# Moving queries, a split output unit, fewer unread products and a finer last step in a two-block decoder kernel

## What is computed

```python
x = x + g1 * even_mixer(mod(rmsnorm(x)), mod(rmsnorm(ctx)))   # gated half + 8 heads over a window and the context
x = x + g2 * (relu(h @ w_ff1) ** 2 @ w_ff2)                   # "mlp 0"
x = x + g1 * conformer_conv(mod(rmsnorm(x)))                  # pw1, gate, 31 taps by depth, layernorm, pw2
x = x + g2 * (relu(h @ w_ff1) ** 2 @ w_ff2)                   # "mlp 1"
x = rmsnorm(x) * final_g
x = x + hybrid_mixer(mod(rmsnorm(x)))                         # 8 block heads, 8 heads over picked keys, w_out_2
x = rmsnorm(x + g2 * peer_ffn(mod(rmsnorm(x)))) * norm_final
```

## Time and profile before

| | |
|---|---|
| median of three executions | 1561.18 us |
| profiled execution, own time | 1555.95 us |
| its span, first to last instruction | 1554.7 us |
| PE busy | 1395.8 us (90%) |
| DVE busy | 1213.7 us (78%) |
| ACT busy | 734.2 us (47%) |
| mean DMA rate over the span | 307 GB/s |
| chain that ended last | PE 58%, DMA 25%, DVE 9%, ACT 4% |

### The profile page before, as it was taken

The page is one execution under the profiler, slowest core; times in us unless marked ns, Lnnn a source line. Parts: engine busy times, 40 slices in busy tenths (PEclk is TensorE's granted clock), DMA queues, the critical chain, the costliest instruction groups (busy, mean ns, idle before and its releaser), DMA issues.

```text
span 1554.7 us, 20828 instructions
## 1 busy us (share of the span) xinstructions
PE 1395.8 (90%) x7582; PEld 1021.0 (66%) x7582; DVE 1213.7 (78%) x2397; ACT 734.2 (47%) x1638; POOL 336.1 (22%) x313
## 2 busy tenths in 40 slices
PE   8999999999999999999999999988777687777776
PEld 3877899998987899998888766543322232222222
DVE  6978888887997788887786799777777777667644
ACT  4555565555485655555354464543333333333323
POOL 1100000001000000003010335455444354434440
PEclk9999999999999999999999999999999999999999
DMA  9854469998420499983432599999999999999996
GB/s 388 318 220 163 158 240 345 351 347 327 167 98 28 173 346 355 343 327 117 155 111 101 188 403 414 380 419 420 419 421 420 421 420 419 421 421 420 420 420 252
DMA packets 66343, 477.15 MB, mean 307 GB/s; under 512 B 7361, under 2 KB 7361, under 8 KB 9153
## 3 DMA queue, kind: packets, MB, share of 16 engines
q0 software_dynamic: 36864, 268.45, 41.9%
q1 hardware_dynamic: 29376, 207.37, 36.0%
q10 hardware_dynamic: 2, 0.01, 0.0%
HBM read 474.75 MB, written 1.05 MB: 306 GB/s over the span
## 4 chain that ended last, share of the span: by engine, by line
PE 58%; DMA 25%; DVE 9%; ACT 4%; issue 2%; POOL 2%; ACTq 0%; DVEq 0%; POOLq 0%
DMA ring<-in_uv,crow 15%; PE ps L2149 8%; PE ps L1732 8%; PE ps L1734 7%; PE ps L1733 7%; DMA row_w<-in_uv,crow 4%; PE ps L2027 4%; PE ps L2026 4%; PE ps L2024 4%; DMA HID<-in_uv,crow 4%; PE ps L2048 3%; DMA row_x<-in_uv,crow 2%; DVE ring L1125 2%; PE ps L1718 1%; DVE WB L496 1%
## 5 line engine op out<-in xcount | busy, mean ns | idle before, releaser
L496 DVE TENSOR_TENSOR WB<-ring,WB 128x1024 fp32r<-128x1024 f32 x229 | 284.1, 1242 | 49.4 <-ACT WB L1212 47.1
L1212 ACT ACTIVATE WB<-ring 128x1024 fp32r<-128x1024 f32 x229 | 240.6, 1052 | 119.6 <-PE ps L2027 85.1
L1732 PE MATMUL ps<-hH,WB 128*128 128x256 f32 x928 | 270.2, 291 | 5.5 <-DVE WB L496 2.8
L2149 PE MATMUL ps<-ring,P 128*128 128x512 f32 x456 | 214.3, 616 | 57.6 <-ACT P L1547 57.6
L1734 PE MATMUL ps<-hH,WB 128*128 128x256 f32 x928 | 263.1, 284 | 0.0
L1733 PE MATMUL ps<-hL,WB 128*128 128x256 f32 x928 | 263.1, 283 | 0.0
L2149 PEld LDWEIGHTS ps<-ring,P 128*128 128x128 f32 x456 | 85.1, 195 | 182.3 <-ACT P L1547 93.5
L1125 DVE CUSTOM_DVE_ANT_0 ring<-ring,cT 128x1024 f32<-128x1024 f32 x114 | 138.3, 1225 | 67.8 <-DMA ring<-in_uv,crow 66.5
L1537 ACT ACTIVATE On<-On 128x2 f32<-128x2 f32 x127 | 25.7, 203 | 344.1 <-DVE On L1125 343.9
L1732 PEld LDWEIGHTS ps<-hH,WB 128*128 128x128 f32 x928 | 178.5, 192 | 10.7 <-issue 6.5
L481 DVE CUSTOM_DVE_ANT_0 ring<-ring,crow,cols 128x1024 f32<-128x1024 f32 x128 | 163.7, 1281 | 26.6 <-DMA ring<-in_um 26.3
(11 more groups left out here) (330 smaller groups left out, 2738.9 us busy)
## 6 DMA issues: line engine op xcount, KB each, us to landing
ring<-in_stream SPq DMA_DIRECT2D x114, 1024.0 KB, 6.8
ring<-in_um SPq DMA_DIRECT2D x66, 1024.0 KB, 7.6
ring<-in_wm SPq DMA_DIRECT2D x4, 1024.0 KB, 15.0
bias<-in_bias SPq DMA_DIRECT2D x2, 2048.0 KB, 15.3
HID<-in_um SPq DMA_DIRECT2D x4, 512.0 KB, 18.6
ring<-in_uv,crow POOLq DMA_INDIRECT x114, 27.7
xT<-in_xT SPq DMA_DIRECT2D x1, 1024.0 KB, 9.0
cT<-in_cxT SPq DMA_DIRECT2D x1, 1024.0 KB, 15.3
```

The source lines that it names most:

```text
L496: ve.tensor_tensor(unit_dst(j, 1), unit_src(j), f(unit_dst(j, 0)), ALU.subtract).then_inc(s_lo, 1)
L1212: se.activation(unit_dst(j, 0), unit_src(j), ACT.Copy).then_inc(s_hi, 1)
L1732: te.matmul(o, wh[:, c], hi[:, kt, :], start=(kt == 0), stop=False)
L2149: mm = te.matmul(ps[4 + 2 * n + q][:, :], diag[:, g % 8, :], row_ap[row_of[g]][:, 1024 + q * 512:1536 + q * 512], start=(g % 128 == 0), st ...
```

## The change

- Expert layer: G1 is 80; the queries 6 to 15 come after lots 3, 6, 9, 13, 16, 20, 23, 27, 31, 35. The routing steps go into the lots of `route_lots` (two of three lots from 5 to 34), and `chosen` follows them. The four transposes of x into xN go in two twos (lots 38 and 42, copied by ACT in 40 and 44); the row of g2 is made at lots 45 to 53.
- Second attention: `cat_lo` of the "B" heads stands at the start of DVE's step j = e + 4, ahead of that step's score. The unit `("w_out2", 0, 2)` is done half in step 15, half in step 16, and DVE adds it to x in step 16.
- Unread products: 6, 6, 5, 5, 5, 5 (x0, mlp0, conv, mlp1, b2, ffn).
- First attention: PE mixes the gate's first half at the end of step 11, and DVE takes its four pieces there. One `mods` leaves step 11 and stands behind the split of `("w_out", 1, 1)`.
- The last two lots: ACT makes one gelu per row, and DVE makes the diagonal from identity, gelu and share in one instruction, right behind the dot.

```diff
+        beside[unit_at["w_in", 0, 3]], beside[first["w_out", 1] + 1] = 0, 1
-        NROW, G1 = 14, 50
-        query_lot = dict(zip(range(6, 16), (3, 4, 6, 8, 10, 12, 14, 16, 18, 20)))
+        NROW, G1 = 14, 80
+        query_lot = dict(zip(range(6, 16), (3, 6, 9, 13, 16, 20, 23, 27, 31, 35)))
+        route_lots = [l for l in range(128) if l < 5 or 5 <= l < 35 and l % 3
+                      or 35 <= l < 40 or l >= 40 and l % 8 < 5]
+        chosen_at = {route_lots[5 * (r - 1) + 2] + 1: r for r in range(1, 16)}
...
                 for j in range(20):
+                    for (a, n), e in LAST.items():
+                        if j == e + 4 and a == "B":
+                            cat_lo(att[a]["base"], n, ps[4 + n][:, :], (a, n))
...
-                        if j == e + 3 + (a == "B"):
+                        if j == e + 3 and a == "C":
                             cat_lo(att[a]["base"], n, ps[4 + n][:, :], (a, n))
...
+            def gate_pieces(n):
+                p = row_bank(("gmix", n))
+                V.wait_ge(*g_mix[n])
+                V.wait_ge(s_bsp, 16)
+                for g in range(4):
+                    c = slice(g * 128, g * 128 + 128)
+                    V.then_inc(ve.scalar_tensor_tensor(out=gsq[n][:, c], in0=p[:, c], scalar=col["lng"][:, g:g + 1],
+                                                       in1=bsp[:, c], op0=ALU.mult, op1=ALU.add))
...
-                    early = i <= 4 or i in (11, 14, 15)
+                    early = i <= 4 or i in (14, 15)
...
+                if i == 11:
+                    gate_pieces(0)
...
-                if w == "w_out2":
+                if w == "w_out2" and j != 15:
                     out2(0, u)
+                if j == 16:
+                    out2(0, 2)
...
-                    if i or l == 127:
+                    if i or l >= 126:
                         ins.then_inc(s_dot, 1)
+                    if l >= 126:
+                        V.wait_ge(s_gel, g - 251)
+                        V.wait_ge(s_gate, 16)
+                        V.wait_ge(s_mix, g - 7)
+                        ve.tensor_scalar(diag[:, g % 8, :], ident[:], dots[:, h, k0 + i:k0 + i + 1],
+                                         gates_[:, h, k0 + i:k0 + i + 1], ALU.mult, ALU.mult).then_inc(s_dgl, 1)
...
-                if l < 15 or l > 15 and l % 8 < 5:
+                if l in route_lots:
                     next(route, None)
...
-            stand_in(ps[2], xT[:, 0:2, :], 7)
+            stand_in(ps[2], xT[:, 0:2, :], 6)
...
-            stand_in(ps[3], cols[:, 0:512], 7)
+            stand_in(ps[3], cols[:, 0:512], 5)
...
+                elif j == 15:
+                    out2_rows(0, 2, parts=(0,))
                 elif w:
                     out2_rows(0, u, (lambda: turn_out("C", 1)) if j == 18 else None)
+                if j == 16:
+                    out2_rows(0, 2, parts=(1,))
...
-                    T.wait_ge(s_dg, g + 1)
+                    T.wait_ge(*((s_dg, g + 1) if l < 126 else (s_dgl, g - 251)))
```

More of the change, by code:

```diff
@@ L715, in into_x @@
                         out_v.then_inc(ins, name)
+            def gate_pieces(n):
[6 more added lines that the diff above has]
+                                                       in1=bsp[:, c], op0=ALU.mult, op1=ALU.add))
             def aside_a(i):
                 if i == 12:
-                    for n in range(2):
-                        p = row_bank(("gmix", n))
-                        V.wait_ge(*g_mix[n])
-                        V.wait_ge(s_bsp, 16)
-                        for g in range(4):
-                            c = slice(g * 128, g * 128 + 128)
-                            V.then_inc(ve.scalar_tensor_tensor(out=gsq[n][:, c], in0=p[:, c], scalar=col["lng"][:, g:g + 1],
-                                                               in1=bsp[:, c], op0=ALU.mult, op1=ALU.add))
+                    gate_pieces(1)
                 if i == 13:
@@ L1552, in gelu_last @@
                     k, g = k0 + i, 2 * l + i
-                    S.wait_ge(s_dot, l + i + 1)
-                    S.then_inc(se.activation(dots[:, h, k:k + 1], dots[:, h, k:k + 1], ACT.Gelu))
-                    S.wait_ge(s_gate, 8 * n + h + 1)
-                    S.wait_own()
-                    S.then_inc(se.activation(wts[:, h, k:k + 1], dots[:, h, k:k + 1], ACT.Copy, scale=gates_[:, h, k:k + 1]))
-                    S.wait_own()
-                    S.wait_ge(s_mix, g - 7)
-                    se.activation(diag[:, g % 8, :], ident[:], ACT.Copy, scale=wts[:, h, k:k + 1]).then_inc(s_dg, 1)
+                    S.wait_ge(s_dot, g - 125)
+                    se.activation(dots[:, h, k:k + 1], dots[:, h, k:k + 1], ACT.Gelu).then_inc(s_gel, 1)
             def finish_last():
@@ L1599, in act @@
             for l in range(128):
-                (gelu if l < 127 else gelu_last)(l)
+                (gelu if l < 126 else gelu_last)(l)
                 if l - 1 in query_at:
@@ L1606, in act @@
                         key_scores(k // 2)
-                if l == 26:
+                if l in (40, 44):
                     S.wait_ge(*dense[used[-1]])
-                    for t in range(4):
+                    for t in (0, 1) if l == 40 else (2, 3):
                         S.wait_ge(s_xnp, t + 1)
@@ L1614, in act @@
                     se.activation(sums[:, 62:63], sums[:, 62:63], ACT.Sqrt).then_inc(s_msr, 1)
-                if l in (3, 8, 13):
-                    chosen(l // 5 + 1)
-                if l % 8 == 3 and 16 < l and l // 8 + 2 < 16:
-                    chosen(l // 8 + 2)
+                if l in chosen_at:
+                    chosen(chosen_at[l])
             finish_last()
@@ L1856, in out_rows, with out2_rows @@
                         between()
-            def out2_rows(half, u, between=None):
+            def out2_rows(half, u, between=None, parts=(0, 1)):
                 i = unit_at["w_out2", half, u]
@@ L1865, in out2_rows @@
                     T.wait_ge(*cat_l["BC"[half], n])
-                for o in range(2):
+                for o in parts:
                     one = apart(half, u)
@@ L1962, in pair_steps, with gate_mix @@
                     yield
+            def gate_mix(n):
+                T.wait_ge(s_wsp, 16)
+                T.wait_ge(g_norm, 1)
+                name = ("gmix", n)
+                T.wait_ge(*empty(row_tiles[row_at[name] - 2]))
+                for g in range(4):
+                    c = slice(g * 128, g * 128 + 128)
+                    mm = te.matmul(row_bank(name)[:, c], gel[:, 4 * n + g, :], wsp[:, c], start=True, stop=True)
+                g_mix.then_inc(mm, n)
             def between_a(i):
                 if i == 12:
-                    T.wait_ge(s_wsp, 16)
-                    T.wait_ge(g_norm, 1)
-                    for n in range(2):
-                        name = ("gmix", n)
-                        T.wait_ge(*empty(row_tiles[row_at[name] - 2]))
-                        for g in range(4):
-                            c = slice(g * 128, g * 128 + 128)
-                            mm = te.matmul(row_bank(name)[:, c], gel[:, 4 * n + g, :], wsp[:, c], start=True, stop=True)
-                        g_mix.then_inc(mm, n)
+                    gate_mix(1)
                 for w, b, u in fill.get(i, ()):
@@ L1988, in between_a @@
                         out_rows(0, u, (lambda: turn_out("A", 1)) if i == 17 else None)
+                if i == 11:
+                    gate_mix(0)
             T.wait_ge(s_const, 4)
@@ L2190, in pe_ @@
                         key_scores(query_at[l] // 2)
-                if l == 24:
+                if l in (38, 42):
                     T.wait_ge(s_hn, 4)
-                    for t in range(4):
+                    for t in (0, 1) if l == 38 else (2, 3):
                         if t >= 2:
```

14 lines of the change are left out of this document (8 added, 6 removed).

## The result

| | before | changed |
|---|---|---|
| median, first measurement | 1561.22 us (1559.51 to 1563.14) | 1547.66 us (1547.12 to 1548.53) |
| median, second measurement | 1560.74 us (1556.74 to 1563.05) | 1547.14 us (1546.70 to 1547.40) |
| profiled execution, own time | 1555.95 us | 1547.12 us |
| its span | 1554.7 us | 1545.5 us |

A forecast was written before the change was run, and what follows sets the result against it. PE bounds the kernel up to about 890 us, then the gathers' DMA near 420 GB/s. Terms -3.6 - 2.0 - 1.3 + 0.2 - 0.1 - 0.5 = -7.3 us take the median from 1561.2 to 1553.9 us; range 1548.5 to 1560.5.

The forecast's parts named there:

- The expert layer: Gathers: spreading the queries, with G1 80, ends the lost transfer around 970 to 1010 us; -3.6 us, bounds 0 and -4.5.
- The unread products: Norms: fewer calls save 1.2 us in ffn, 0.6 in mlp1, 0.2 in conv; -2.0 us, bounds -3.9 and 0.
- Score and sum: Second attention, step 12: XB ready sooner, -1.3 us; bounds -1.3 and -2.8, the latter if the clock's fall there goes.
- The halved unit: Second attention, last turn: score 15 stays behind a split, gap over 1.5 us; division late, +0.2 us, bounds -1.5 and +0.5.
- The last two lots: End of the gathers: the last weight load starts sooner by a quicker diagonal; -0.5 us, bounds 0 and -0.7.
- The gate: First attention: PE's unit 1.0 us sooner, moved `mods` loses 0.9 of 1.28 us; -0.1 us, bounds -1.0 and +1.0.
- The rival of the clock: Four norms: fewer unread products let the clock fall, 1.7 us each, 6.8 in all; 1560.7 us, 8%.
- carried over, the median becomes: Whole kernel: the profiled execution's 5.2 us below the median was kept, giving 1561.2 - 7.3 = 1553.9 us.
- Eight buffers that starve row sets 50 to 80: Gathers: late mixes hold that stretch at 380 GB/s, 7.1 us lost, old 3.6 us stay; 1564.6 us, 8%.
- the prediction's signs: Signs included first gather 2 to 4 us sooner, and no stretch under 410 GB/s after the gathers' first 70 us.
- A loss that only moves: Gathers: the lost transfer stays, only elsewhere, so the queries' term is 0; 1557.5 us, 13%.
- The halved unit fills its gap: Second attention, ahead of the last turn: score 15 can come 1.5 us sooner, 1.7 us more gained; 1552.2 us, 8%.

The follow-up runs named there:

- e7: The changed kernel with the low half of the B heads behind score and maximum again: median 1549.37 us.
- e6: The changed kernel with the unit (0, 2) whole in step 15 again: median 1551.20 us.
- e5: The changed kernel with the gate's halves mixed together in step 12 again and its modulation dot back in step 11: median 1549.80 us.
- e0: The kernel before, unchanged, measured again with a second profile: median 1559.93 us, profiled execution 1559.19 us.
- e4: The changed kernel, unaltered, measured again with a second profile: median 1547.14 us.
- e9: The changed kernel with the counts of unread products of before (7, 6, 6, 6, 6, 7): median 1549.71 us.
- e11: The changed kernel with unit (0, 2) whole in step 15 and two calls of unread products in PE's gap ahead of the last turn: 1547.83 us.

## Why the prediction was right, and short

The sum was right, nearly term by term, where the terms were made of waits and durations; what it lacks is the clock, twice. The direction and the causes of these terms hold. With the clock left out, the measured median fell outside the stated range.

*Right.* The expert layer: forecast -3.6, -3.59 by the dots, 2.8 in the median with that part alone. The two stretches at 970 us show the cause. The unread products: forecast -2.0 with its division by norm, measured -1.85 by trace and +2.0 to +2.6 when put back. Score and sum: 1.32 us of PE's wait, forecast 1.3, and 1.36 us when taken back (e7). The halved unit: that score 15 stays where the split leaves it, and the turn's gap over 1.5 us, was seen as forecast. The last two lots: -0.74 for -0.5; the bound was -0.7. The gate, -0.16 for -0.1 in an execution without a fall, is near by luck: the moved dot cost 0.42 us where 0.9 was forecast, and PE reached the mean 0.59 us sooner (187.79 before, 187.20 after, both ahead of the wait) where 1.0 was.

*Short, first step.* "Unit (0, 2) in two halves: +0.2, bounds -1.5 and +0.5." It is -4.1 in the median (e6), outside the bounds. The step asked what the turn waits for and found, rightly, that no product in front of it makes it start sooner. It didn't ask what the clock does behind a gap that PE enters after 2.1 us of short operations; my evidence that a 1.65 us gap costs no clock was one execution, and it was one of the two of five that had their fall at 828 us instead. The gate's step has the same flaw: -0.1, bounds -1.0 and +1.0, measured -2.7 (e5), outside them too. The rival of the clock was in the list, but with the sign turned: I looked for falls that the change would bring by taking unread products away, and priced only one, at 828 us, that it would spare.

*Short, second step.* "It stood 5.2 us below the median of the executions shown; carried over, the median becomes ..." The two kernels don't share that distance. It was 5.2 for before and is 0.5 for the changed kernel. This makes up 4.7 of the 6.3 us by which the forecast fell short; 1.5 more is the spared fall at 828 us, which stood in the prediction as a bound. What made most executions of before longer than the profiled one is read from the second profile and from e5 and e6: falls at 157 and 847 us, which the gate's and the unit's parts take away. Second profile against second profile (e0, e4), the changed kernel is 12.6 us ahead: 7.4 up to the first dot, 4.4 in the gathers, 0.7 behind the last dot. The timed executions without a trace can't be divided like this.

*The rivals.* Eight buffers that starve row sets 50 to 80: there is a sag in that place, and it is small. The rate is 408 GB/s at 1045 to 1065 in the changed kernel, 20 x (420 - 408)/420 = 0.6 us, not 7.1; that the eight buffers cause it wasn't tested. (Of the prediction's signs two are missed by little: the first dot came 4.87 us sooner, not 2 to 4, and this stretch is under 410 GB/s.) A loss that only moves: no, the dots span 3.59 us less. A clock that falls at the norms: no. The halved unit fills its gap: by effect yes, by mechanism no, since the gap stayed.

*Open.* The term-by-term effects taken back one at a time (2.7, 4.1, 2.2, 2.0 or more) with 3.6 and 0.7 make over 15 us, more than the 13.6 of the whole. A spared fall may be counted with more than one part: the profiles of e5, e7 and e9 have the fall near 885 us, both of the changed kernel don't. Nor was the last two lots' part run alone; its 0.74 us rest on the traces: 11.2 us behind the last dot in the five profiles without it, 10.5 in the nine with it. And whether a gap brings a fall is read off 14 profiles, one execution each; only e5, e6 and e11 tie a fall to a change in the median.

## What to carry to other kernels

Ask of each gap of PE not only who ends it but what PE did in the microseconds ahead of it: a wait among short operations can cost, by the clock behind it, more than twice its own length (4.1 us for 1.65 in e6), and filling it with unread products bought back 3.4 of these (e11), real products 4.1. A fall that is spared in one place can come in the next: look at the whole stretch. When single executions of a kernel spread by more than the effects in question, one profile is one draw: read the timed executions' spread first, and never carry the distance from profile to median over to the changed kernel.

## What the runs showed of the hardware

The granted clock went from 1.00 (2.4 GHz) to half (1.2 GHz) behind short waits. At 157 us, with the gate late (e5), these were 1.16 and 0.63 us of idle among QK, turn and value products,

```profile
148.00:156.00 8.00, 6.61 (x43) 4.77 (x43) 6.44 (x17) 5.62 (x11) 0.00 (x0) 1.00 0.40 142
```

with PE busy for 6.61 of the 8 us ahead of the fall. The changed kernel has the same operations there and 7.63 us busy, and in nine profiles of kernels with that order the clock never fell. Once down it stayed there for 3.4 us (e0 at 157), 6.8 (e5) or 10.2 (e6), though PE was busy for 6.37 of 7 us and 9.76 of 10.5 in these stretches. One and the same program had a fall in one execution and not in the other, with the same work ahead of it. At 828 us the first profile of before fell and e0 didn't; the 8 us ahead, first before, then e0:

```profile
820.00:828.00 8.00, 6.27 (x48) 5.63 (x47) 4.07 (x8) 5.16 (x12) 0.00 (x0) 1.00 0.31 103
```

```profile
820.00:828.00 8.00, 6.27 (x48) 5.64 (x47) 4.78 (x8) 4.45 (x12) 0.00 (x0) 1.00 0.19 56
```

By the Trainium skill ("TensorE: Matmul & The Clock Gate", Part 1) the throttled state is the default and activity releases it; e11, where unread products in the gap keep the clock at 1.00 in place of 0.51, agrees with that. A fall cost 0.3 to 0.45 of its length: 1.0 us for 3.4 at 157, 3.0 for 6.8 at 847 (e0), 4.1 for 10.2 at 842 (e6).
